# First attention: the last head's values projected two units later, early output tiles begun two units later with two parts in each unit

## The chip, the cores and the metric

The kernel runs on one core of one Trainium2 chip. The metric is the device time of one execution in microseconds (us). TensorE (PE), VectorE (DVE), ScalarE (ACT) and GpSimd (POOL) run their own instruction lists and wait for one another on semaphores; SyncE (SP) issues the loads.

## The reference, cut to what matters

The reference computes two transformer layers with feed-forward halves, on 256 context and 256 latent tokens of width 1024, and then a third layer of another kind. In order: half FFN, differential attention, half FFN; half FFN, grouped attention, half FFN; FFN, a layer with dilated and block attention, FFN. The change touches the attention parts, the first above all:

```python
q, k, v = project(h); qc, kc, vc = project(hc)
q, k = apply_rope(q, cos, sin), apply_rope(k, cos, sin)
k_all = concatenate([kc, k], axis=1); v_all = concatenate([vc, v], axis=1)
sc = einsum('blhid,bkhid->bihlk', qb, kb) * scale        # two maps i for each of 8 heads
p = softmax(sc, axis=-1)
p = p[:, 0] - lam_full * p[:, 1]
o = einsum('bhlk,bkhd->blhd', p, vb)
o = rmsnorm(o, subln) * (1.0 - lambda_init)
y = o @ w_out
```

## The kernel before, in words

All weights stream from HBM once, as tiles of 128 x 1024 f32, through a ring of 6 slots. ScalarE copies each tile to a rounded `w_hi` (L796), GpSimd subtracts to get `w_lo` (L776), and every product is three matmuls, hi x hi, lo x hi and hi x lo (L1589, L1590, L1593). A load into a slot waits until the tile six places earlier has been used.

The first attention (kind "da") has 24 items, q, k and v of 8 heads, one weight tile each, 8 chunks of k. An item is projected in four parts of two chunks (6 matmuls over 512 tokens). There are 32 units, four for each head, one for each block of 128 queries: blocks of latents attend to 512 keys (long), blocks of the context to 256 (short). Heads 0 to 6 take them long, short, long, short; the last head takes two long and then two short ones. Unit U goes through these steps:

- S(U), L1905: scores of the two maps on TensorE, into the same two PSUM banks for every unit, so S(U) waits until the exponentials of U-1 are done. VectorE takes the maximum (L1505) and scales it (L1507), ScalarE the exponentials (L1055).
- C(U), L1408 to L1420: VectorE combines the two maps to `pcomb`.
- T(U), L1918: TensorE transposes `pcomb`, ScalarE copies it to `probT` (L1061).
- PV(U), L1938: TensorE multiplies by the values.
- After a head's units: O (square on ScalarE L1073, `o_raw` on VectorE L1519), oss (sum of squares on TensorE L1968, its root on ScalarE), on (L1536, `o_hi` L1088) and ol (`o_lo`, L1540).

A projected item is evacuated by ScalarE (L1028); q and k then need a rope, rot on TensorE (L1873) and three operations on VectorE (L1475 to L1478); v needs vtr, transposes on TensorE (L1879) and a copy on VectorE to `v_st` (L1482). ScalarE's evacuation of tile t is followed by the `w_hi` copy of tile t+4.

`mixer_plan` (L139) writes one list for an attention before anything is issued, and every engine goes through this list in the same order. Step U of its loop puts down T(U-2), C(U-1), S(U), PV(U-2), and between them projection parts, as many as `QUOTA[kind][U]` says, in thirds: ahead of S, ahead of PV, after PV. Where a unit has no projection part, it places as many early parts as `FILLS[kind][U]` says: two chunks of the output projection of output tiles 0 and 1 (kind "early"), whose sums are left open in PSUM banks 0 and 1. These are also the banks of the items, so the first early part waits for evacuations (L1943). A rope or a transpose is put down when the planner's clock, one tick for each part, has reached its due time, or at the latest ahead of the S or PV that needs it. The list before, from unit 24 (for L1905 and the others each name is one step; `k7.4` is the part of item k, head 7, chunks 4 and 5; `E02` is the early part of output tile 0, chunks 2 and 3; `E06` and `E16` are one chunk each):

```
24: T22 C23 ol4 | q7.4 | S24 | q7.6 | PV22
25: T23 C24 | k7.0 | S25 | k7.2 | rot q7 | PV23 O5 | k7.4
26: T24 C25 | k7.6 | oss5 | S26 on5 | v7.0 | PV24 | v7.2 | rot k7
27: T25 C26 ol5 | v7.4 | S27 | v7.6 | PV25
28: T26 C27 | E00 | S28 | PV26
29: T27 C28 | E10 | vtr v7 | S29 | PV27 O6
30: T28 C29 | E02 | S30 | E12 | oss6 | PV28
31: T29 C30 | E04 | S31 on6 | E14 | PV29 ol6 O7
32: T30 C31 | E06 | PV30
33: T31 | E16 | oss7 on7 ol7 | PV31 O7'
```

T28 and T29 on ScalarE are each followed by the `w_hi` copy of output tile 4 and 5. After the list comes the output projection. The second attention ("ga", 12 items, of which the last is q of head 7 with a norm whose squares ScalarE makes, L1021) and the third ("b2", 30 items) use the same planner.

Of the kernel before, what the change touches and what calls it, by code (L numbers as in the profile page):

```python
# [131 lines left out]

GA_ORDER = [("k", 0), ("v", 0), ("q", 0), ("q", 1), ("k", 1), ("q", 2), ("v", 1)] + [("q", h) for h in range(3, GA_HEADS)]
LEAD = {"da": 4, "ga": 9}
QUOTA = {"da": [3, 3, 3, 3] + [3, 3, 2] * 8, "ga": [2, 2, 3, 3, 3] + [2] * 7}
FILLS = {"da": [0] * 28 + [1, 1, 2, 2, 1, 1], "ga": [0] * 12 + [2, 2, 1, 1, 1, 1], "b2": [0] * 21 + [3, 3, 3, 3, 3]}


def mixer_plan(kind, t0):  # L139
# [51 lines left out]
    order, turns, ropes, norms, clock, pending = [], 0, 0, 0, 0, []  # L191
# [42 lines left out]
    def add_part(part):  # L234

        nonlocal clock
        add("proj", part)
        clock += 1
        it, _, k1 = part
        if k1 == CH:  # L240
            if it["norm"] or it["rope"] or it["what"] == "v":
                pending.append(("ss" if it["norm"] else "rot" if it["rope"] else "vtr", it, clock + (1 if it["norm"] else 2)))

    def prepare(n):
        op, it, _ = pending.pop(n)
# [28 lines left out]
    every = sorted((it for st in sets for it in st["items"]), key=lambda it: it["idx"])  # L274
# [29 lines left out]
    for U in range(len(units) + LAG):  # L304
# [4 lines left out]
        if u:  # L309
            st = u["set"]  # L310
            n, nu = U - st["first_unit"], len(st["units"])
            if kind == "b2":
                nxt = parts(st["s"] + 1)
                mine = nxt[n * len(nxt) // nu:(n + 1) * len(nxt) // nu]
            elif U < len(QUOTA[kind]):
                mine, stream = stream[:QUOTA[kind][U]], stream[QUOTA[kind][U]:]
        fills = FILLS[kind][U] if not mine else 0
        third = -(-len(mine) // 3)
# [45 lines left out]
def build(nc, A):  # L364
# [97 lines left out]
    ident, rot = tab[:, 0:128], tab[:, 128:256]  # L462
# [1114 lines left out]
    def _(pe):  # L1577
# [246 lines left out]
        def mixer(b):  # L1824
            kind = b["kind"]
            S = MS[kind]
            order, n_items, n_first = plans[kind]
# [16 lines left out]
            for op, x, turn in order:  # L1844
                if op == "first":
                    first_phase(b, [(it["t"], item_bank(it, n_first), it["tok"]) for it in x])
                elif op == "proj":
                    x, k0, k1 = x
# [13 lines left out]
                elif op == "ss":  # L1862
                    pe.wait_ge(S["proj_evac"], x["idx"] + 1)
                    turn_wait(turn)
                    mm(psum[:, TURN[turn % 2], x["tok"]], ones[:, :], n_sq[:, x["sq"] % 2, x["tok"]], start=True, stop=True)\
                        .then_inc(S["turn_ready"], 1)
                elif op == "rot":
                    if x["norm"]:
                        pe.wait_ge(S["normed"], x["norm_n"])
                    else:  # L1870
                        pe.wait_ge(S["proj_evac"], x["idx"] + 1)
                    turn_wait(turn)
                    mm(psum[:, TURN[turn % 2], 0:SEQ], rot, latents(x), start=True, stop=True).then_inc(S["turn_ready"], 1)  # L1873
                elif op == "vtr":
                    pe.wait_ge(S["proj_evac"], x["idx"] + 1)
                    turn_wait(turn)
                    src = item_stage(x)
                    for kt in range(width(x["tok"]) // 128):
                        last = nc.tensor.transpose(psum[:, TURN[turn % 2], kt * 128:(kt + 1) * 128],  # L1879
                                                   src[:, kt * 128:(kt + 1) * 128], ident)  # L1880
                    last.then_inc(S["turn_ready"], 1)
                elif op == "S":
                    U, st, n = x["U"], x["set"], x["keys"]
                    if U == 0:
                        pe.wait_ge(S["proj_evac"], n_first)
                    for it in st["q"] + st["k"]:
                        if U == st["first_unit"]:
                            item_ready(it)
                    if kind == "b2":
                        if U >= 2:  # L1890
                            pe.wait_ge(S["biased"], freed[U - 2])
                        biased += len(st["v"])
                        freed[U] = biased
                    elif U >= lag_of(kind):
                        pe.wait_ge(S["exp_done"], exps_through(kind, U - lag_of(kind)))
                    out = scores_of(kind, x)
                    if kind == "ga":
                        q = latents(st["q"][0])[:, x["qt"] * 128 - CTX:x["qt"] * 128 - CTX + 128]
                        k0 = place_of(st["k"][0])
                        last = mm(out, q, k_st[:, k0:k0 + n], start=True, stop=True)  # L1900
                    elif kind == "da":
                        for m in range(2):
                            rows = slice(64 * m, 64 * m + 64)
                            q0, k0 = place_of(st["q"][0]) + x["qt"] * 128, place_of(st["k"][0])
                            last = mm(out[:, m, :], q_st[rows, q0:q0 + 128], k_st[rows, k0:k0 + n], start=True, stop=True)  # L1905
                    else:
                        queries = (q_st, q_odd)[x["j"]]
                        for g in range(len(st["v"])):
                            q0, k0 = place_of(st["q"][g]) + x["qt"] * 128, place_of(st["k"][g])
                            last = mm(out[:, g * n:g * n + n], queries[:, q0:q0 + 128], k_st[:, k0:k0 + n],  # L1910
                                      start=True, stop=True)
                    last.then_inc(S["s_ready"], 1)
                elif op == "T":
                    u, a, e = x
                    pe.wait_ge(S["pc_ready"], u["U"] + 1)
                    turn_wait(turn)
                    for n in range(a, e):
                        last = nc.tensor.transpose(psum[:, TURN[turn % 2], (n - a) * 128:(n - a + 1) * 128],  # L1918
                                                   pcomb[:, u["U"] % 2, n * 128:(n + 1) * 128], ident)
                    last.then_inc(S["turn_ready"], 1)  # L1920
                elif op == "PV":
                    st, U = x["set"], x["U"]
                    done = x["turns"] + [it["turn"] for it in st["v"]]
                    for bank in range(2):
                        if any(n % 2 == bank for n in done):
                            pe.wait_ge(*turn_freed(S, max(n for n in done if n % 2 == bank)))
                    if U == st["first_unit"] and st["s"]:
                        if kind == "ga":
                            if st["s"] > 1:
                                pe.wait_ge(S["olo_ready"], st["s"] - 1)  # L1930
                        elif kind == "da":
                            pe.wait_ge(S["o_evac"], st["s"])
                            pe.wait_ge(S["osq_ready"], st["s"])
                        else:
                            pe.wait_ge(S["olo_ready"], st["s"])
                    for n, (g, kt) in enumerate(x["blocks"]):
                        half = FULL if kind != "da" else LAT if x["qt"] >= 2 else slice(0, CTX)
                        last = mm(psum[:, pv_bank(kind, st["s"], half), x["ocol"]:x["ocol"] + 128], v_tile(st["v"][g], kt),  # L1938
                                  probT[:, U % 2, n * 128:(n + 1) * 128], start=n == 0, stop=n == len(x["blocks"]) - 1)
                    last.then_inc(S["pv_ready"], 1)  # L1940
                elif op == "early":
                    d, k0, k1 = x
                    if d + k0 == 0:  # L1943
                        pe.wait_ge(S["proj_evac"], n_items)
                    if kind == "b2":
                        t = b["t_body"] + 30 + d
                        last = blocks(t % RING if k0 else split(t), psum[:, d, 0:SEQ], normed(FULL_U), range(k0, k1), first=k0,
                                      start=k0 == 0, stop=k1 == CH)
                        if k1 == CH:
                            last.then_inc(tile_used, 1)  # L1950
                    else:
                        t = b["t_out"] + d
                        pe.wait_ge(S["olo_ready"], k1)
                        tok = b["tok_out"]
                        bank = next(bank for j, _, bank in b["pieces"] if j == d)
                        blocks(t % RING if k0 else split(t), psum[:, bank, tok],
                               lambda k: (o_hi[:, k, tok], o_lo[:, k, tok]), range(k0, k1), first=k0, start=k0 == 0, stop=False)
                elif op == "oss":
                    if x["n"] < DA_HEADS:
                        oss((op, x, turn))  # L1960
# [151 lines left out]
```

## Time and profile before

| | |
|---|---|
| median of 3 runs | 2390.12 us (2389.14 to 2393.72) |
| profiled execution | 2389.94 us |
| its span | 2388.1 us |
| PE busy, share of the span | 2315.0 us (97%) |
| PEld, DVE, ACT, POOL busy | 2069.3, 1306.9, 974.7, 1338.8 us |
| first attention's PV steps | 461.3 to 647.7 us of the span |

The span reaches from the first to the last instruction of the profiled execution. A row of the timeline has its start, its duration, engine, source line, output and inputs, and in brackets the idle time of the engine ahead of it and who ended that. Matmuls overlap, so the pitch from one start to the next is what one costs, not its duration.

### The profile page before, as it was taken

The page shows a single profiled execution, that of the slowest core. Times are in us where ns is not written, and L with a number is a line of the kernel's source. Part 1 is how long each engine was busy: PE and PEld are TensorE (multiplying, and loading weights), DVE is VectorE, ACT ScalarE, POOL GpSimd, SP SyncE. Part 2 cuts the span into 40 slices and gives each one's busy share as a digit, 9 for nine tenths or more (in the row PEclk, how much of TensorE's full clock was granted, in tenths as well). Part 3 has the DMA queues.
Part 4 walks back from the last instruction along what each step waited for, and adds up shares of the span by engine and source line. Part 5 has one row for each costly group of instructions (what it writes and reads, how often), then busy time and mean ns, then how long its engine had stood idle before and what let it go on. Part 6 is the DMA issues. An engine that isn't in the chain of part 4 may idle for free.

```text
span 2388.1 us, 36102 instructions
## 1 busy us (share of the span) xinstructions
PE 2315.0 (97%) x14528; PEld 2069.3 (87%) x14528; DVE 1306.9 (55%) x2196; ACT 974.7 (41%) x1605; POOL 1338.8 (56%) x700
## 2 busy tenths in 40 slices
PE   7999999999889999999999999899999999999998
PEld 5888889777688888899888897799999999999998
DVE  8898296666678982967332036564324315533331
ACT  4322224455442322244223235455445444555443
POOL 4564465222135654654444443178878887468886
PEclk9999999999999999999999999999999999999999
DMA  6555362211025553624553331145545564345554
GB/s 271 212 190 180 110 219 85 71 62 54 28 79 212 194 177 110 219 94 178 194 176 110 97 102 62 45 158 185 179 149 196 176 188 163 106 152 184 183 178 134
DMA packets 97509, 350.09 MB, mean 147 GB/s; under 512 B 10945, under 2 KB 10945, under 8 KB 96961
## 3 DMA queue, kind: packets, MB, share of 16 engines
q1 hardware_dynamic: 97344, 347.81, 43.2%
q8 instruction: 115, 1.88, 0.3%
q14 instruction: 50, 0.40, 0.1%
HBM read 346.71 MB, written 1.05 MB: 146 GB/s over the span
## 4 chain that ended last, share of the span: by engine, by line
PE 60%; DVE 5%; ACT 2%; issue 2%; DMA 1%; POOL 1%; SPq 0%; DVEq 0%; ACTq 0%
PE psum L1589 19%; PE psum L1593 19%; PE psum L1590 19%; POOL w_lo L776 1%; ACT w_hi L796 1%; PE psum L1938 1%; DMA w_raw<-in_ffn_out 0%; DVE stat L1505 0%; DVE psum L1141 0%; DVE psum L1221 0%; DVE h L1227 0%; PE psum L1910 0%; DVE pcomb L1414 0%; DVE u_lo L1445 0%; ACT prob L1055 0%
## 5 line engine op out<-in xcount | busy, mean ns | idle before, releaser
L776 POOL TENSOR_TENSOR w_lo<-w_raw,w_hi 128x1024 fp32r<-128x1024 f32 (+3 forms) x696 | 1338.6, 1945 | 1032.3 <-ACT w_hi L796 1031.7
L1589 PE MATMUL psum<-u_hi,w_hi 128*128 128x256 f32 (+2 forms) x2912 | 973.9, 334 | 12.1 <-POOL w_lo L776 8.2
L1593 PE MATMUL psum<-u_lo,w_hi 128*128 128x256 f32 (+2 forms) x2912 | 948.7, 326 | 3.3 <-DVE u_lo L1213 2.0
L1590 PE MATMUL psum<-u_hi,w_lo 128*128 128x256 f32 (+2 forms) x2912 | 947.4, 325 | 0.0
L796 ACT ACTIVATE w_hi<-w_raw 128x1024 fp32r<-128x1024 f32 (+1 forms) x522 | 537.3, 1032 | 439.9 <-PE psum L1593 345.1
L1589 PEld LDWEIGHTS psum<-u_hi,w_hi 128*128 128x128 f32 x2912 | 555.2, 191 | 75.3 <-issue 24.4
L1593 PEld LDWEIGHTS psum<-u_lo,w_hi 128*128 128x128 f32 x2912 | 554.6, 190 | 51.8 <-DVE u_lo L1213 3.8
L1590 PEld LDWEIGHTS psum<-u_hi,w_lo 128*128 128x128 f32 x2912 | 555.5, 191 | 45.3 <-issue 3.4
L1589 PE MATMUL psum<-gu_hi,w_hi 128*128 128x256 f32 (+1 forms) x1188 | 379.3, 319 | 1.0 <-POOL w_lo L776 1.0
L1590 PE MATMUL psum<-gu_hi,w_lo 128*128 128x256 f32 (+1 forms) x1188 | 378.2, 318 | 0.0
L1593 PE MATMUL psum<-gu_lo,w_hi 128*128 128x256 f32 (+1 forms) x1188 | 378.1, 318 | 0.0
L1589 PEld LDWEIGHTS psum<-gu_hi,w_hi 128*128 128x128 f32 x1188 | 226.3, 191 | 17.0 <-issue 1.4
L1590 PEld LDWEIGHTS psum<-gu_hi,w_lo 128*128 128x128 f32 x1188 | 226.3, 191 | 15.8
L1593 PEld LDWEIGHTS psum<-gu_lo,w_hi 128*128 128x128 f32 x1188 | 226.3, 191 | 15.4
L1141 DVE CUSTOM_DVE_ANT_0 psum<-ada_hi,silu_c,col 128x1024 f32<-128x1024 f32 x80 | 155.4, 1942 | 54.6 <-DMA ada_hi<-in_ada_w 50.8
L948 ACT ACTIVATE sq<-psum 128x512 f32<-128x512 f32 x66 | 39.5, 598 | 324.7 <-PE psum L1593 175.1
L1141 DVE CUSTOM_DVE_ANT_0 psum<-ada_lo,silu_c,col 128x1024 f32<-128x1024 f32 x80 | 148.6, 1857 | 33.2 <-DMA ada_lo<-in_ada_w 28.7
L1318 DVE TENSOR_TENSOR gu_lo<-sq,gu_hi 128x512 fp32r<-128x512 f32 (+1 forms) x132 | 147.1, 1115 | 18.3 <-ACT gu_hi L933 18.3
L1350 DVE TENSOR_TENSOR sq<-sq,psum 128x512 f32<-128x512 f32 (+1 forms) x110 | 63.7, 579 | 162.3 <-PE psum L1593 157.2
L1237 DVE TENSOR_TENSOR rstd<-rstd,sq 128x256 f32<-128x256 f32 (+1 forms) x58 | 45.1, 778 | 182.1 <-ACT sq L892 90.2
L1141 DVE CUSTOM_DVE_ANT_0 psum<-ada_out,silu_c,col 128x1024 f32<-128x1024 f32 x64 | 134.8, 2168 | 0.1
L1055 ACT ACTIVATE prob<-psum,stat 128x512 f32<-128x512 f32 (+1 forms) x80 | 47.6, 599 | 103.3 <-DVE stat L1507 103.1
(180 smaller groups left out, 1989.2 us busy)
## 6 DMA issues: line engine op xcount, KB each, us to landing
w_raw<-in_ffn_in SPq DMA_DIRECT2D x264, 512.0 KB, 3.5
w_raw<-in_ffn_out SPq DMA_DIRECT2D x96, 448.0 KB, 3.4
ada_hi<-in_ada_w SPq DMA_DIRECT2D x48, 512.0 KB, 5.2
ada_lo<-in_ada_w SPq DMA_DIRECT2D x48, 512.0 KB, 5.2
w_raw<-in_ffn_out SPq DMA_DIRECT2D x48, 512.0 KB, 3.6
ada_out<-in_ada_w SPq DMA_DIRECT2D x32, 512.0 KB, 3.8
w_raw<-in_b_qkv SPq DMA_DIRECT2D x30, 512.0 KB, 3.4
w_raw<-in_da_in SPq DMA_DIRECT2D x24, 512.0 KB, 3.5
```

The costliest lines, as they stand in the source:

```text
L776: last = pool.tensor_tensor(w_lo[:, slot, w], w_raw[:, slot, w], w_hi[:, slot, w].bitcast(F32), ALU.subtract)
L796: scalar.activation(w_hi[:, slot, 0:cols], w_raw[:, slot, 0:cols], ACT.Copy).then_inc(hi_ready, 1)
L948: scalar.activation(s_up[:, j, tok], psum[:, pair_bank(m), tok], ACT.Silu).then_inc(silu_ready, 1)
L1055: scalar.activation(prob[:, U % 2, m * 512:m * 512 + n], src, ACT.Exp, bias=stat[:, U % 4, 2 + m:3 + m], scale=scale, accum_out=stat[:, U ...
L1141: return vec.tensor_tensor_reduce(out=psum[:, junk:junk + 2, :].rearrange("p a b -> p (a b)"), in0=tile, in1=silu_c[:, c, :], scale=1.0, s ...
L1237: vec.tensor_tensor(sqsum[:, tok], sqsum[:, tok], sq[:, i % 2, tok], ALU.add).then_inc(yacc_ready, 1)
L1318: vec.tensor_tensor(gu_lo[:, m, tok], s_up[:, m % 2, tok], gu_hi[:, m, tok].bitcast(F32), ALU.subtract)\
L1350: vec.tensor_tensor(s_up[:, j, tok], s_up[:, j, tok], psum[:, pair_bank(m) + 1, tok], ALU.mult)\
L1589: mm(out, w_hi[:, slot, w], x_hi, start=start and n == 0, stop=False)
L1590: mm(out, w_lo[:, slot, w], x_hi, start=False, stop=False)
L1593: last = mm(out, w_hi[:, slot, w], x_lo, start=False, stop=stop and n == len(ks) - 1)
L1938: last = mm(psum[:, pv_bank(kind, st["s"], half), x["ocol"]:x["ocol"] + 128], v_tile(st["v"][g], kt), probT[:, U % 2, n * 128:(n + 1) * 12 ...
```

## The change

The last two units of projection move from 26 and 27 to 28 and 29, with fewer parts in units 22 to 27; the eight early parts move to units 30 to 33, two in each. The very last item's rope or transpose is due one tick after its last part and not two. The first early part of tile 0 waits for all items but the last, that of tile 1 for all. The last two edits act on all three attentions.

```diff
-QUOTA = {"da": [3, 3, 3, 3] + [3, 3, 2] * 8, "ga": [2, 2, 3, 3, 3] + [2] * 7}
-FILLS = {"da": [0] * 28 + [1, 1, 2, 2, 1, 1], "ga": [0] * 12 + [2, 2, 1, 1, 1, 1], "b2": [0] * 21 + [3, 3, 3, 3, 3]}
+QUOTA = {"da": [3, 3, 3, 3] + [3, 3, 2] * 6 + [2, 3, 2] + [2, 2, 1] + [2, 2], "ga": [2, 2, 3, 3, 3] + [2] * 7}
+FILLS = {"da": [0] * 30 + [2, 2, 2, 2], "ga": [0] * 12 + [2, 2, 1, 1, 1, 1], "b2": [0] * 21 + [3, 3, 3, 3, 3]}
...
-                pending.append(("ss" if it["norm"] else "rot" if it["rope"] else "vtr", it, clock + (1 if it["norm"] else 2)))
+                pending.append(("ss" if it["norm"] else "rot" if it["rope"] else "vtr", it, clock + (1 if it["norm"] or it is every[-1] else 2)))
...
                 elif op == "early":
                     d, k0, k1 = x
-                    if d + k0 == 0:
-                        pe.wait_ge(S["proj_evac"], n_items)
+                    if k0 == 0:
+                        pe.wait_ge(S["proj_evac"], n_items - 1 + d % 2)
```

## Rows read from the trace of the kernel before

**Rows 1.** The page: busy time of TensorE and the others, share of the span, instructions.

```profile
PE 2315.0 (97%) x14528; PEld 2069.3 (87%) x14528; DVE 1306.9 (55%) x2196; ACT 974.7 (41%) x1605; POOL 1338.8 (56%) x700
```

**Rows 2.** Windows at the first attention's end: length, busy us (instructions) of PE, PEld, DVE, ACT, POOL.

```profile
582.00:620.00 38.00, 38.00 (x190) 27.48 (x188) 24.59 (x52) 20.02 (x46) 9.92 (x4) 1.00 0.18 56
620.00:648.00 28.00, 22.37 (x120) 15.98 (x119) 16.30 (x33) 14.09 (x36) 7.06 (x3) 1.00 0.06 19
```

**Rows 3.** Timeline of TensorE, 620 to 648 us: the four longest waits (start, duration, line).

```profile
621.13 0.50 PE L1589 MATMUL psum<-o_hi,w_hi 128*128 128x512 f32 x1 [1.01 <-ACT vT L1028]
...
631.85 0.70 PE L1905 MATMUL psum<-k_st,q_st 64*128 64x256 f32 x4 [1.35 <-ACT prob L1055]
...
636.76 0.66 PE L1918 MATMUL psum<-tab,pcomb 128*128 128x128 f32 x4 [0.87 <-DVE pcomb L1420]
...
644.27 0.50 PE L1589 MATMUL psum<-o_hi,w_hi 128*128 128x512 f32 x1 [2.15 <-DVE o_lo L1540]
```

**Rows 4.** Timeline of TensorE, 602 to 611 us: steps of units 25 and 26, read as pitches.

```profile
602.81 0.70 PE L1905 MATMUL psum<-k_st,q_st 64*128 64x256 f32 x4
603.44 0.50 PE L1589 MATMUL psum<-u_hi,w_hi 128*128 128x512 f32 x1
...
604.94 0.59 PE L1873 MATMUL psum<-q_st,tab 128*128 128x256 f32 x2
605.37 0.61 PE L1938 MATMUL psum<-probT,v_st 128*128 128x128 f32 x4
...
607.56 0.48 PE L1589 MATMUL psum<-u_hi,w_hi 128*128 128x512 f32 x1
...
609.04 1.02 PE L1968 MATMUL psum<-o_sq,ones 128*128 128x512 f32 x2
609.99 1.13 PE L1905 MATMUL psum<-k_st,q_st 64*128 64x512 f32 x4
611.05 0.50 PE L1589 MATMUL psum<-u_hi,w_hi 128*128 128x512 f32 x1
```

**Rows 5.** Timeline of VectorE, 615 to 637 us: a rope, two combinations, a copy, an o_raw.

```profile
615.46 0.42 DVE L1475 TENSOR_TENSOR rope_a<-k_st,tab 128x256 f32<-128x256 f32 x1 [1.60 <-PE psum L1873]
...
616.26 0.42 DVE L1478 TENSOR_TENSOR k_st<-rope_a,rope_b 128x256 f32<-128x256 f32 x1
...
617.38 0.75 DVE L1420 SCALAR_TENSOR_TENSOR pcomb<-prob,stat 128x512 f32<-128x512 f32 x1
...
628.30 0.68 DVE L1482 COPY v_st<-psum 128x512 f32<-128x512 f32 x1
...
632.38 0.75 DVE L1519 TENSOR_SCALAR o_raw<-psum,col 128x512 f32<-128x512 f32 x1 [2.06 <-ACT o_sq L1073]
...
633.83 2.88 DVE L1420 SCALAR_TENSOR_TENSOR pcomb<-prob,stat 128x512 f32<-128x512 f32 x1
```

**Rows 6.** Timeline of GpSimd: one subtraction by itself, two in a row.

```profile
633.80 2.36 POOL L776 TENSOR_TENSOR w_lo<-w_raw,w_hi 128x1024 fp32r<-128x1024 f32 x1 [9.34 <-ACT w_hi L796]
...
660.15 4.92 POOL L776 TENSOR_TENSOR w_lo<-w_raw,w_hi 128x1024 fp32r<-128x1024 f32 x2 [16.48 <-ACT w_hi L796]
```

**Rows 7.** Timeline of ScalarE, 619 to 632 us: exponentials, evacuation, weight copy, exponentials, square.

```profile
619.57 0.47 ACT L1055 ACTIVATE prob<-psum,stat 128x256 f32<-128x256 f32 x1 [3.51 <-DVE stat L1507]
...
620.49 0.59 ACT L1028 ACTIVATE vT<-psum 128x512 f32<-128x512 f32 x1
620.96 1.06 ACT L796 ACTIVATE w_hi<-w_raw 128x1024 fp32r<-128x1024 f32 x1
...
630.35 0.69 ACT L1055 ACTIVATE prob<-psum,stat 128x512 f32<-128x512 f32 x1 [3.27 <-DVE stat L1507]
...
631.69 0.59 ACT L1073 ACTIVATE o_sq<-psum 128x512 f32<-128x512 f32 x1
```

**Rows 8.** Timeline of TensorE in the second attention: its first early part.

```profile
1531.17 0.39 PE L1589 MATMUL psum<-o_hi,w_hi 128*128 128x256 f32 x1 [1.28 <-ACT n_sq L1021]
```

**Rows 9.** Timeline of VectorE in the third attention, unit 21: the last values' copy.

```profile
2097.42 0.42 DVE L1482 COPY v_st<-psum 128x256 f32<-128x256 f32 x1
```

## Prediction

> **What bounds the kernel now.** I read the page's busy shares first: TensorE is busy for 2315.0 of 2388.1 us [rows 1], at full clock. A change that only reorders work can win at most TensorE's idle time near the reordered steps. So next, the windows around the end of the first attention: from 582 to 620 us TensorE has no idle time at all; from 620 to 648 us it is busy 22.37 of 28.00 us, so 5.6 us are idle [rows 2]. Then the timeline of TensorE there: four waits make most of it [rows 3]. The first early output part waits 1.01 us for the evacuation of the last head's values (all 24 items must be evacuated); S(30) waits 1.35 us for the exponentials of unit 29; T(29) waits 0.87 us for pcomb(29); the early part (0, 6..7) waits 2.15 us for head 6's low half. Thus 5.6 us is the whole prize here: 0.23% of the run.
>
> **What the change does to the order.** With the new quotas (2,3,2,2,2,1,2,2 parts in units 22 to 29) the planner's loop gives, written as in the list of the order before (E06 is the early part of tile 0 from k=6): unit 26 is T24 C25 | k7.2 | rot q7 | S26 | k7.4 | oss5 | PV24; unit 27 is T25 C26 | k7.6 | S27 | on5 | PV25; unit 28 is T26 C27 ol5 | v7.0 | rot k7 | S28 | v7.2 | PV26; unit 29 is T27 C28 | v7.4 | S29 | v7.6 | PV27 O6; unit 30 is T28 C29 | E00 | vtr v7 | S30 | E10 | oss6 | PV28; unit 31 is T29 C30 | E02 | S31 | on6 | E12 | PV29 ol6 O7; unit 32 is T30 C31 | E04 | E14 | oss7 on7 ol7 | PV30; and the last is T31 | E06 | E16 | PV31 O7', before the output. No instruction is added or removed on any engine. Four parts leave units 22 to 27; units 28, 29, 32 and 33 hold two parts each instead of one. The last key head's rope now comes right ahead of S28, which needs it; before, it came in unit 26.
>
> **Units 22 to 27: 6.0 us earlier.** One part takes 1.50 us after an S (603.44 to 604.94) and 1.48 elsewhere (607.56 to 609.04) [rows 4]. Walking the list with those pitches (S 0.63 on two key tiles, 1.06 on four, rot 0.43, oss 0.9), T26 comes at 613.5 instead of 619.5. The softmax chain keeps up: exponentials last 0.92 us (two key tiles) or 1.34 (four) [rows 7], and each is done 0.3 us or more before the next S. T24 to T26 find pcomb ready. So 4 x 1.5 us is carried to unit 28, as work still to be done.
>
> **Unit 28: a new wait.** v7.0 and rot k7 end at 615.8. S28 needs k7's rope, and VectorE has C27 and ol5 queued in front of it. C27 needs exp27. Those stand behind k7.6's evacuation and the head copy of a weight tile on ScalarE (0.60 and 1.06 us) [rows 7]: they run 614.05 to 615.1. That same copy releases a w_lo subtraction on GpSimd of 2.4 us, 614.1 to 616.5, or to 616.85 if on5 holds it up first. Here is a row that decides much: pcomb(29) took 2.88 us instead of 0.75 [rows 5], and ended just after GpSimd's w_lo, which ran 633.80 to 636.16 [rows 6]. An operation of VectorE with its operands in SBUF waits for GpSimd. So C27 stands until 616.85, ends at 617.7; ol5 takes 0.65, the rope 1.2 [rows 5], and S28 starts at 619.55. TensorE idles 3.7 us. Bounds: without GpSimd in the way C27 ends at 616.1, S28 starts at 618.0 and the idle is 2.1; the rope can't be avoided. I take 3.7, since the copy always stands directly ahead of exp27, and 2.4 us outlast the 1.0 us of exp27.
>
> **Units 29 and 30: a second new wait.** S28 619.55, v7.2, PV26, T27 623.0, v7.4, S29 624.7 (exp28 ends 623.6), v7.6 to 627.3, PV27. On ScalarE: exp29 627.3 to 628.8, evacuation of v7 to 629.3, weight copy to 630.35, o_sq6 to 630.8, probT28, a second copy to 632.35. GpSimd so runs two w_lo back to back, 630.4 to 635.3. T28 at 627.75, E00 (now waiting for 23 items only; free), vtr v7 at 629.65, S30, E10, oss6: TensorE has work to 633.2. But VectorE takes o_raw6 (0.75 us [rows 5], ends 631.5), C29, and only then the copy of v7's transposes, which PV28 needs. C29's four operations need SBUF: the first gets in between the two w_lo, the rest wait for 635.3 and end 636.4; the copy takes 0.68 [rows 5] to 637.05. PV28 starts then, 3.8 us idle. If all of C29 slips in between the two w_lo, PV28 starts at 634.85: 2.2 us less. With GpSimd out of the way in both units PV28 starts near 632.05, 5.0 us less.
>
> The page of the Trainium skill "SBUF — State Buffer", section "Who interferes with whom", calls the shared port pair an exclusive lock, held for the whole instruction by whoever issues first. The trace agrees: two w_lo took 4.92 us without a gap to speak of [rows 6]. By that rule C29's waiting operation goes first, the second w_lo next, and the others behind it, which is the 636.4 above; were the port shared by bandwidth instead, C29 would end near 634 and the sum would be some 2.2 us lower.
>
> **Units 31 to 33.** PV28 637.05, T29 637.95, E02, S31 639.9 (exp30 ends 638.9), E12, PV29 642.0, T30 642.9, E04, E14, oss7 646.0, PV30, T31 646.85 (C31 ends 646.7), E06, E16 to 648.5. ol6 is blocked to 644.6 by a third w_lo, as in the trace, but E06 is now late enough: the 2.15 us wait goes. The 0.87 and 1.35 waits go too. PV31 waits for probT31 behind oss7's two activations and o_hi7: 648.7. The output starts at 649.1, against 647.7; as o_sq of the last piece is ready in time, the fifth chunk starts at 650.9, which is 0.8 us late against the trace. Counted by idle time it is more: 3.7 + 3.8 + 0.2 after, less the 5.6 before, is 2.1; the pitches that I rounded down lie between. I take **+1.0 us**: what the filler covers in units 30 to 33 it uncovers in 28 and 30. The rest of the output is the same list; its tile loads (two of them after tiles 0 and 1 are released) move with it.
>
> **The other two attentions.** The first early part's wait is relaxed in all three. In the second attention it waits 1.28 us for q7's squares [rows 8]; now it runs at once (0.82 us of matmuls, to 1530.5), and the sum of squares behind it waits for them instead, until 1531.15 and not 1531.99: **-0.8 us**, bounds 0 (if a chain behind it is bound elsewhere) and -0.84. In the third, nothing waits there. The rule for the last values' transpose ("due one step sooner") acts there too: v5's transposes pass S(21), so VectorE's copy of 0.42 us [rows 9] now precedes that unit's softmax; that delay finds slack except behind exp23, where PV22 already waits for probT: **+0.3 us**, bounds 0 and 0.42.
>
> Sum: 1.0 - 0.8 + 0.3 = +0.5 us on the profiled execution's 2389.94 us (its span of 2388.1 and 1.8 around it): 2390.4. The median of the three runs is 2390.12, 0.2 above that execution, so the forecast is 2390.6 us. The three runs differ by 4.6 us among themselves, and 0.2% is 4.8 us: a smaller change can hardly be told from none.
>
> **Rivals.**
> A. GpSimd costs less than I take. For it: only one pcomb in the four units of the tail is caught in the trace, the rest escape. Against: both copies stand right ahead of the exponentials. With the second collision softened 2390.6 - 2.2 = 2388.4; with both gone (PV28 at 632.05) 2390.6 - 5.0 = 2385.6.
> B. Slower. In unit 27 the scaling of the maximum (a two-element operation in SBUF) starts at 613.8, GpSimd's w_lo at 614.1. If it comes 0.3 us later it stands until 616.5, exp27 ends 617.5, S28 starts 620.55: +1.0, so 2391.6. It decides once S27 slips by 0.3 us against k7.6's evacuation; for it, the margin is so small; against, both hang on the same last matmul of k7.6.
> C. The waits simply fill: two parts in each of the last units cover the chains, nothing new waits, and the 5.6 us idle go but for 0.5: 2390.1 - 5.1 - 0.5 = 2384.5. Against it: the rope right ahead of S28.
> D. The reordering has no effect and only the relaxed wait counts: 2389.3. The quotas do move v7, so this is thin.
>
> **Chances.** Forecast 0.48, A 0.25, B 0.18, C 0.07, D 0.02. Faster by over 0.2% needs C or the far end of A: 0.09. Slower by over 0.2% needs B and a further 3.5 us: 0.05. Within 0.2%: 0.86. Range: A's near end and some of its far end, B and the runs' own spread above: 2386.5 to 2393.0.
>
> **What will show it.** Right if the trace has: T26 near 613.5; an idle of 2 to 4 us ahead of S28, released by the rope's last addition on VectorE; one of 2 to 4 us ahead of PV28, released by v_st's copy, with C29 stretched; no wait ahead of E06; in the second attention E00 starting before 1530 and the sum of squares waiting for n_sq. Wrong if S28 starts without a wait, if PV28 finds v7 ready, or if units 22 to 27 show an idle of their own, which would mean that the parts taken out of them were cover.

## The result: 0.18% slower, and the profile after

| | before | after |
|---|---|---|
| median, 12 runs each | 2389.24 us | 2394.54 us |
| lowest to highest | 2386.84 to 2393.72 | 2390.47 to 2396.26 |
| ratio, 95% interval | | 1.0018 [1.0010, 1.0026] |
| profiled execution | 2389.94 us (span 2388.1) | 2396.26 us (span 2394.4) |
| mean granted clock of the profiled execution | 0.997 | 0.994 |

The forecast was 2390.6 us (2386.5 to 2393.0), most likely "within 0.2%". The time is 5.3 us over before and 1.5 us above the range. A second build of the changed kernel, run later, gave 2394.3 us (1.0020 [1.0011, 1.0029]).

The profile's busy line answers to [rows 1]. TensorE does the same 14528 matmuls and is "busy" 5.8 us longer.

```profile
PE 2320.8 (97%) x14528; PEld 2073.1 (87%) x14528; DVE 1302.9 (54%) x2196; ACT 975.0 (41%) x1605; POOL 1340.5 (56%) x700
```

That is the first hint: reordering alone would show as idle time, not as busy time. The windows show where. Columns as in [rows 2]; the seventh value behind the window's name, after the five engines, is the granted clock (1.00 is 2.4 GHz, 0.50 is 1.2 GHz).

```profile
620.00:648.00 28.00, 22.76 (x93) 16.14 (x94) 14.50 (x26) 10.34 (x22) 6.33 (x3) 0.82 0.05 19
622.00:624.00 2.00, 2.00 (x5) 0.50 (x5) 0.14 (x1) 0.00 (x0) 0.00 (x0) 0.50 0.03 8
624.00:626.00 2.00, 2.00 (x5) 1.57 (x6) 1.25 (x2) 0.68 (x2) 0.00 (x0) 0.50 0.00 0
626.00:628.00 2.00, 2.00 (x10) 1.85 (x9) 1.13 (x4) 0.77 (x4) 0.00 (x0) 0.52 0.00 0
628.00:630.00 2.00, 2.00 (x12) 1.46 (x13) 0.35 (x1) 0.39 (x1) 0.00 (x0) 1.00 0.00 0
640.00:642.00 2.00, 0.23 (x1) 0.24 (x2) 1.97 (x4) 0.00 (x0) 0.04 (x1) 0.89 0.00 0
642.00:644.00 2.00, 2.00 (x10) 2.00 (x11) 0.84 (x5) 1.45 (x5) 0.00 (x0) 0.50 0.00 0
644.00:646.00 2.00, 2.00 (x10) 1.61 (x8) 0.71 (x2) 1.97 (x4) 0.00 (x0) 0.76 0.00 0
```

Before, this window stood at 1.00 with 120 matmuls [rows 2]; now it holds 93 in about the same busy time. The clock is at 0.50 from about 621 to about 628 us, so it fell while TensorE was still waiting, and again from about 642 to 645.

What TensorE did before each fall is in its timeline. It answers to [rows 3]: none of the four waits of before is left, and two of 3.5 us are new. (S, T, PV and E are the steps of the list.)

```profile
617.63 0.59 PE L1873 MATMUL psum<-k_st,tab 128*128 128x256 f32 x2
621.74 2.08 PE L1905 MATMUL psum<-k_st,q_st 64*128 64x512 f32 x4 [3.52 <-DVE k_st L1478]
623.75 0.80 PE L1589 MATMUL psum<-u_hi,w_hi 128*128 128x512 f32 x1
624.35 0.63 PE L1590 MATMUL psum<-u_hi,w_lo 128*128 128x512 f32 x1
...
626.48 1.74 PE L1938 MATMUL psum<-probT,v_st 128*128 128x128 f32 x8
628.05 0.38 PE L1918 MATMUL psum<-tab,pcomb 128*128 128x128 f32 x2
...
641.76 2.08 PE L1938 MATMUL psum<-probT,v_st 128*128 128x128 f32 x8 [3.50 <-DVE v_st L1482]
643.63 1.06 PE L1918 MATMUL psum<-tab,pcomb 128*128 128x128 f32 x4
...
646.21 0.70 PE L1905 MATMUL psum<-k_st,q_st 64*128 64x256 f32 x4
```

S(28) takes 2.08 us where S(29), of the same shape, takes 1.13. From the start of S(28) to T(27) it is 6.31 us (621.74 to 628.05); in a kernel below with the same list and a full clock there it is 3.43 (fill28, 621.21 to 624.64). From PV(28) to S(31) it is 4.45 us, against 2.92 (fill_full, 638.47 to 641.39). That is 2.9 and 1.5 us, 4.4 together.

VectorE and GpSimd show who made the waits. They answer to [rows 5] and [rows 6].

```profile
617.37 0.17 DVE L1408 RECIPROCAL stat<-stat 128x2 f32<-128x2 f32 x1 [0.49 <-ACT prob L1055]
617.57 1.55 DVE L1416 TENSOR_TENSOR stat<-stat,small 128x1 f32<-128x1 f32 x1
...
636.71 1.05 DVE L1416 TENSOR_TENSOR stat<-stat,small 128x1 f32<-128x1 f32 x1
637.68 2.64 DVE L1417 TENSOR_SCALAR prob<-prob,stat 128x512 f32<-128x512 f32 x1
640.36 0.75 DVE L1420 SCALAR_TENSOR_TENSOR pcomb<-prob,stat 128x512 f32<-128x512 f32 x1
```

```profile
616.37 2.75 POOL L776 TENSOR_TENSOR w_lo<-w_raw,w_hi 128x1024 fp32r<-128x1024 f32 x1 [8.53 <-ACT w_hi L796]
635.35 4.68 POOL L776 TENSOR_TENSOR w_lo<-w_raw,w_hi 128x1024 fp32r<-128x1024 f32 x2 [16.24 <-ACT w_hi L796]
```

A multiplication of one element in each partition, in combination 27 (L1416, 0.16 us alone), ends at 619.12, where the first subtraction ends. In combination 29 the second operation ends 0.3 us after the 640.03 at which the two subtractions end.

In the second attention the wait of [rows 8] is gone and a shorter one stands behind it. In the third, the wait of PV(22) is 0.77 us and was 0.64. After:

```profile
1537.04 0.60 PE L1918 MATMUL psum<-tab,pcomb 128*128 128x128 f32 x4
...
1538.93 0.70 PE L1865 MATMUL psum<-n_sq,ones 128*128 128x256 f32 x2 [0.57 <-ACT n_sq L1021]
...
1542.61 0.66 PE L1918 MATMUL psum<-tab,pcomb 128*128 128x128 f32 x4 [0.52 <-DVE pcomb L1414]
...
1548.85 0.39 PE L1589 MATMUL psum<-o_hi,w_hi 128*128 128x256 f32 x1 [1.54 <-DVE o_lo L1524]
...
2110.52 0.71 PE L1938 MATMUL psum<-probT,v_st 128*128 128x128 f32 x4 [0.77 <-ACT probT L1061]
```

The second attention before:

```profile
1529.29 0.60 PE L1918 MATMUL psum<-tab,pcomb 128*128 128x128 f32 x4
...
1541.10 0.39 PE L1589 MATMUL psum<-o_hi,w_hi 128*128 128x256 f32 x1 [1.55 <-DVE o_lo L1524]
```

From the transpose ahead of the relaxed wait to the early part that waits for `o_lo` it is 11.81 us before and 11.81 after. What the relaxed wait gains there, a new wait of 0.52 us for pcomb and the steps around it give back.

**A ruler for the stretch.** Short falls of the clock come in all these kernels at other places too, in the trace of before for instance around 1446 and 1776 us, and they move the end of a run by some us. So I measure the changed stretch by itself: from the start of S(22) to the first operation of the output (`MEMSET rstd`, L1377). Before and after:

```profile
583.54 1.13 PE L1905 MATMUL psum<-k_st,q_st 64*128 64x512 f32 x4
```
```profile
652.83 0.48 DVE L1377 MEMSET rstd<- 128x512 f32 x1
```
```profile
585.13 1.13 PE L1905 MATMUL psum<-k_st,q_st 64*128 64x512 f32 x4
```
```profile
660.00 0.48 DVE L1377 MEMSET rstd<- 128x512 f32 x1
```

That is 69.3 us before and 74.9 after: +5.6 us.

### The profile page after: what moved, and what is told of

Its sections match the earlier page's. It is cut to its first block, busy times and chain, and to the rows that moved or that the text cites. A ratio compares the mean times of both kernels' runs of the same rounds, so it can differ in the third digit from the quotient of the medians.

```text
span 2394.4 us, 36101 instructions
## 1 busy us (share of the span) xinstructions
PE 2320.8 (97%) x14528; PEld 2073.1 (87%) x14528; DVE 1302.9 (54%) x2196; ACT 975.0 (41%) x1605; POOL 1340.5 (56%) x700
## 3 DMA queue, kind: packets, MB, share of 16 engines
HBM read 346.71 MB, written 1.05 MB: 145 GB/s over the span
## 4 chain that ended last, share of the span: by engine, by line
PE 61%; DVE 4%; ACT 2%; issue 1%; POOL 1%; DMA 1%; DVEq 0%; SPq 0%; ACTq 0%
PE psum L1589 20%; PE psum L1593 20%; PE psum L1590 19%; ACT w_hi L796 1%; POOL w_lo L776 1%; PE psum L1938 1%; DVE stat L1505 0%; DVE psum L1221 0%; PE psum L1910 0%; DVE h L1227 0%; DVE pcomb L1414 0%; DVE u_lo L1445 0%; ACT prob L1055 0%; PE psum L1918 0%; DMA w_raw<-in_ga_in 0%
## 5 line engine op out<-in xcount | busy, mean ns | idle before, releaser
L1141 DVE CUSTOM_DVE_ANT_0 psum<-ada_out,silu_c,col 128x1024 f32<-128x1024 f32 x64 | 129.3, 2083 | 0.1
```

What stands on the lines that cost most here:

```text
L1141: return vec.tensor_tensor_reduce(out=psum[:, junk:junk + 2, :].rearrange("p a b -> p (a b)"), in0=tile, in1=silu_c[:, c, :], scale=1.0, s ...
```

## The experiments

The runs were timed in four sets. The medians of the kernel before, in the same sets, were 2389.90, 2389.38, 2389.38 and 2389.58 us. "Stretch" is the ruler above; "clock" says whether the granted clock fell to 0.50 in it.

| kernel | median us | ratio [95%] | wait S(28), PV(28), us | stretch, us | clock |
|---|---|---|---|---|---|
| before_again | 2389.76 | 0.9999 [0.9990, 1.0008] | 0, 0 | 69.3 | no fall |
| after_again | 2394.30 | 1.0020 [1.0011, 1.0029] | 3.52, 3.52 | 73.7 | two falls |
| quota_only | 2397.12 | 1.0028 [1.0018, 1.0039] | 3.52, 3.89 | 77.6 | two |
| wait_only | 2387.97 | 0.9989 [0.9981, 0.9998] | 0, 0 | 69.7 | one |
| fill28 | 2393.59 | 1.0014 [1.0005, 1.0023] | 0.63, 3.50 | 70.5 | no fall |
| fill_both | 2394.50 | 1.0016 [1.0007, 1.0025] | 0.63, 0.63 | 70.5 | no fall |
| fill_both_again | 2393.62 | 1.0017 [1.0008, 1.0026] | 0.62, 0.61 | 70.5 | no fall |
| fill_full | 2393.11 | 1.0013 [1.0004, 1.0022] | 0.18, none | 70.5 | no fall |
| late_k7 | 2390.21 | 1.0003 [0.9994, 1.0013] | 2.11, 3.52 | 73.3 | two |
| late_v7 | 2390.46 | 1.0007 [0.9998, 1.0016] | 3.52, 0 | 69.6 | one |
| late_copies | 2386.71 | 0.9989 [0.9980, 0.9998] | 2.12, 0 | 68.2 | one |
| late_copies_again | 2386.92 | 0.9990 [0.9982, 0.9999] | 2.11, 0 | 66.7 | no fall |
| late_fill | 2386.46 | 0.9985 [0.9977, 0.9994] | 0.33, 0 | 66.7 | no fall |
| late_before | 2389.74 | 0.9999 [0.9990, 1.0008] | 0, 0 | 70.0 | one |

after_again is the changed kernel without an edit. Expected of it were a time 4 to 5 us over before and, if the falls belong to the waits, both falls again; both came.

**1. Is it the clock? Fillers in the waits (fill28, fill_both, fill_both_again, fill_full).** `keep_clock` issues dummy matmuls of 0.24 us each on TensorE.

```diff
                 elif op == "S":
                     U, st, n = x["U"], x["set"], x["keys"]
+                    if kind == "da" and U == 28:
+                        keep_clock(0, 13)
...
                 elif op == "PV":
                     st, U = x["set"], x["U"]
+                    if kind == "da" and U == 28:      # not in fill28
+                        keep_clock(SUMS, 13)
```

> The changed kernel with 13 matmuls of ones (128 columns, 0.24 us a call, 3.2 us in all, into a PSUM bank that nothing uses then) put ahead of S28, inside its wait of 3.5 us. Clock theory: the changed kernel lost 2.8 us because TensorE's granted clock fell to 0.5 after the idle ahead of S28, and 1.6 us in the same way ahead of PV28. With the first wait filled the clock stays at 1.00 through S28, v7.2 and PV26, S28 takes 1.13 us and not 2.08, and the time falls by 2.8 us against the changed kernel, to about 2391.7. Rival, the waits alone: the loss is the 7 us of waits; filling one with work that does nothing changes nothing (2394.5), and the slow matmuls would be slow for another reason.

> The same with 13 more such matmuls ahead of PV28, into the sums' bank, inside its wait of 3.5 us. Clock theory: granted clock 1.00 from 616 to 660 us, 4.4 us less than the changed kernel, about 2390.1, which is what the forecast without a clock loss gave. Rival, the waits alone: 2394.5 still.

> The kernel with fillers ahead of S28 and PV28 once more. Its first median stood 3.7 us over the kernel before, against 1.4 us by the chain of the first attention alone (its stretch was 1.9 us longer in the trace, 4.2 less than in the changed kernel's). Clock theory: it must now lie between, 2 to 4 us under the changed kernel measured beside it. Rival: the falls are exchanged for others elsewhere or hardly occur outside of the trace, and it lies within 1 us of the changed kernel.

> The changed kernel with 15 filler matmuls instead of 13 ahead of S(28) and ahead of PV(28), so that only some 0.2 us of idle time is left at each instead of 0.63. If what is left of the clock's cost hangs on that remaining idle time: the time falls from 2393.6 to 2394.5 us (13 fillers) toward 2390 us. If the fillers bring back the clock but the work still ends late, because the idle time itself is the larger part: 2393 to 2394.5 us again, with a mean granted clock of 0.996 to 0.9965 over the executions as before the change. Longer by over 0.3 us would say that the fillers themselves stand in the way.

The window of fill_full, and its S(28):

```profile
620.00:648.00 28.00, 27.69 (x161) 21.48 (x160) 17.68 (x33) 12.38 (x29) 7.55 (x3) 1.00 0.06 19
```
```profile
621.31 1.13 PE L1907 MATMUL psum<-k_st,q_st 64*128 64x512 f32 x4 [0.18 <-DVE k_st L1478]
```

In the window the clock is 1.00, and S(28) takes 1.13 us. In all four filler traces the stretch is 70.5 us, within 0.03 of one another. The fillers stand inside waits that are there anyway, so this is the change with the clock taken out: 70.5 - 69.3 = **1.2 us**. The rest of the 5.6 us in the profiled execution, 4.4 us, is the clock; in after_again it is 3.2. The mean granted clock over the executions comes back as well: 0.9953 with the change (23 executions), 0.9964 with fillers (45), 0.9967 before (129).

The executions give a second price for the clock. Among the executions of one kernel, 0.001 less of the mean granted clock goes with about 1.3 us more (a straight line through all of them). By this estimate the 0.0014 between before and after are worth 1.8 us; they would be 3.3 us (0.0014 of 2390 us) if all the clock that was lost had been needed. The two traces, with 3.2 and 4.4 us, lie at that upper end and above it.

The medians do not follow. With fillers they lie from 0.2 us above to 1.2 us below the changed kernel's 2394.30, where the expectations of fill28 and fill_both had 2.8 and 4.4 us; even by the estimate above the clock that came back is worth 1.4. By what was written down ahead of these runs, the rival ("the waits alone") has the times, and the clock theory has the traces. fill_full, with 15 fillers, shows that it does not hang on the 0.6 us left idle. One way in which the gain is given back is in the trace of fill_full: just behind the stretch, VectorE's norm meets two subtractions of GpSimd, TensorE waits 3.69 us, and its clock falls to 0.50 there.

```profile
665.08 2.43 DVE L1237 TENSOR_TENSOR rstd<-rstd,sq 128x256 f32<-128x256 f32 x1 [3.61 <-PE psum L1593]
```
```profile
668.00:672.00 4.00, 4.00 (x19) 4.00 (x20) 0.63 (x2) 0.00 (x0) 0.00 (x0) 0.50 0.00 0
```

The same wait is 1.3 to 1.5 us long before and after the change, with no fall behind it in those four traces; in fill_both_again it is 1.79, with a fall. The other two filler traces have neither a wait over 1.6 us nor a fall there, and still their rest of the run takes 1737.3 and 1736.4 us where the changed kernel's takes 1734.4. The mean of the 45 filler executions is 3.8 us over before's, where the idle time (1.2 us here and 0.3 in the third attention) and 0.4 to 0.7 us of clock add up to 2.2 at most. So why the fillers' times stay high is open.

Behind the stretch there is one more fall that the ruler does not see. All 16 traces have a wait of 2.5 to 2.6 us ahead of a norm's sum of squares (L1623, L1627 where lines were added; at 708.9 us in before). In 11 of them a fall follows, in both traces of the changed kernel too, and the 100 us behind the stretch are then 1.2 to 1.7 us longer than in before; in the two traces of before none follows. Whether that is chance or comes with the change, two traces cannot say.

**2. Is the trace of before typical (before_again)?** The same kernel.

> The kernel before, unchanged, for a second trace of it. The stretch from the first half FFN's end to the first attention's end took 358.0 us in the first trace. If that trace was typical: 357 to 359.5 us again and no slow clock within 600 to 660 us. If it was a lucky draw: over 359.5 us, and the part of the loss that idle time explains shrinks by the same amount. Time 2389 to 2390.5 us, ratio 1.000.

The stretch is again 69.3 us, with no fall, and has the same waits within 0.03 us. The +1.2 rests on two traces against four. The time and the stretch came as the first branch expected.

**3. Who makes the waits? The weight copies moved (late_copies).** ScalarE's `w_hi` copies of output tiles 2 to 5 are taken from behind the evacuations of k7 and v7 and from behind T(28) and T(29), and put behind the exponentials of units 28 and 30 and behind T(29) and T(30). GpSimd's subtractions go with them.

```diff
                         scalar.activation(dst, src, ACT.Copy).then_inc(S["proj_evac"], 1)
+                if kind == "da" and x["idx"] >= 22:
+                    return
                 refill(x["t"])
...
+                    if kind == "da" and U in (28, 30):
+                        heads_to(b["t_out"] + {28: 2, 30: 3}[U])
...
-                    if kind == "da" and u["set"]["s"] == DA_HEADS - 1:
-                        heads_to(min(b["t_out"] + 4 + u["U"] - u["set"]["first_unit"], b["t_out"] + RING - 1))
+                    if kind == "da" and u["U"] in (29, 30):
+                        heads_to(b["t_out"] + {29: 4, 30: 5}[u["U"]])
```

> The changed kernel with four of ScalarE's weight copies moved (and so GpSimd's subtractions): output tile 2's from k7's evacuation to behind the exponentials of unit 28, tile 3's to behind those of unit 30, tiles 4 and 5's behind probT29 and probT30. Theory: GpSimd held C27 (first SBUF pair operation 1.55 us instead of 0.16) and C29 (1.05 + 2.64 us instead of 0.16 + 0.48). Without that, S28 waits 2.1 us instead of 3.5 and PV28 0.5 instead of 3.5; if the clock stays up after waits that short, the time falls by 4.4 + 4.4, to about 2386; if it still falls ahead of S28, to about 2388.5. Rival: the order itself (rope and copy behind the combination) makes the waits, and they stay over 3 us each: 2394.5.

> The changed kernel with all four weight copies moved, a second time. If the first result (2386.7 us, 0.9989 of before) was the kernel and not the draw of the clock: 2386 to 2388 us, ratio under 1.0 again, S(28) waits 2.1 us for the rope, PV(28) does not wait. If it was the draw: near before, 2389.5 us.

VectorE in the second trace: combination 27, the rope's last addition, combination 29 and the copy of the values.

```profile
615.70 0.16 DVE L1420 TENSOR_TENSOR stat<-stat,small 128x1 f32<-128x1 f32 x1
615.78 0.34 DVE L1421 TENSOR_SCALAR prob<-prob,stat 128x256 f32<-128x256 f32 x1
...
617.95 0.42 DVE L1482 TENSOR_TENSOR k_st<-rope_a,rope_b 128x256 f32<-128x256 f32 x1
...
629.79 0.16 DVE L1420 TENSOR_TENSOR stat<-stat,small 128x1 f32<-128x1 f32 x1
629.87 0.48 DVE L1421 TENSOR_SCALAR prob<-prob,stat 128x512 f32<-128x512 f32 x1
...
631.05 0.68 DVE L1486 COPY v_st<-psum 128x512 f32<-128x512 f32 x1
```

And what TensorE still waits for:

```profile
618.47 1.13 PE L1909 MATMUL psum<-k_st,q_st 64*128 64x512 f32 x4 [2.11 <-DVE k_st L1482]
...
643.51 0.44 PE L1922 MATMUL psum<-tab,pcomb 128*128 128x128 f32 x2 [1.67 <-DVE pcomb L1424]
```

No operation of the combinations is held, PV(28) finds its values, and what is left ahead of S(28) is the rope itself, 2.11 us. The stretch is 66.7 us without a fall, 2.5 under before; the median is 7.6 and 7.4 us below the changed kernel's 2394.3, and 3.2 and 2.5 below before. So the two waits that GpSimd makes, with what follows them, are more than the whole loss.

**4. One collision or two (late_k7, late_v7)?** late_k7 moves the copy of tile 2 alone, late_v7 those of tiles 3 to 5 alone. The edit of late_k7:

```diff
+                if kind == "da" and x["idx"] == 22:
+                    return
                 refill(x["t"])
...
+                    if kind == "da" and U == 28:
+                        heads_to(b["t_out"] + {28: 2}[U])
```

> Only the weight copy of output tile 2 is moved, from k7's evacuation to behind the exponentials of unit 28; the other copies stay as in the changed kernel. Theory (two separate collisions with GpSimd, each followed by a slow clock if the idle time is long): the wait ahead of S(28) falls from 3.5 to about 2.1 us, pcomb(27) runs 0.75 us instead of 1.55 and unstretched by GpSimd; the wait ahead of PV(28) stays at 3.5 us with two subtractions in a row. Time 1.4 us below the changed kernel if the clock is unaffected, up to 4 us below where the clock no longer falls behind S(28): 2390.5 to 2393 us against 2394.3. Rival (one collision carries all): if this one, 2387; if the other, no change, 2394.3.

> Only the weight copies of output tiles 3, 4 and 5 are moved, from v7's evacuation and from behind units 28 and 29 to behind the exponentials of unit 30 and T(29), T(30); tile 2's copy stays where the changed kernel has it. Theory: the wait ahead of S(28) stays at 3.5 us; the wait ahead of PV(28) falls from 3.5 us to under 1 us, since combination 29 no longer stands behind GpSimd; 3 us less from idle time and up to 1.6 us from the clock: 2389.7 to 2391.3 us. Rival (the k7 collision carries all): 2394. The sum of this gain and that of the kernel with tile 2's copy alone should be near the 7 us that moving all gave.

They take 4.1 and 3.8 us off the changed kernel's 2394.3; together that is 7.9, and moving all took 7.4 to 7.6. Two separate collisions, about equal, and both needed. The stretch without a fall is 70.5 with both and 66.7 with neither, 3.8 us in idle time. The other half of the 7.5 us of the medians is beyond idle time. The clock's 3.2 to 4.4 in the traces would cover it; by the mean granted clock (0.9968 in the 22 executions with all copies moved, 0.9953 with the change) it is 2 us, up to 3.5. In late_k7's trace, too, the clock falls twice:

```profile
620.74 1.54 PE L1909 MATMUL psum<-k_st,q_st 64*128 64x512 f32 x4 [2.11 <-DVE k_st L1482]
639.45 2.07 PE L1942 MATMUL psum<-probT,v_st 128*128 128x128 f32 x8 [3.52 <-DVE v_st L1486]
```

**5. Which edit does it (quota_only, wait_only)?** quota_only is the kernel before with the two lines `QUOTA` and `FILLS` of the change; wait_only is the kernel before with the relaxed wait of the early parts alone:

```diff
-                    if d + k0 == 0:
-                        pe.wait_ge(S["proj_evac"], n_items)
+                    if k0 == 0:
+                        pe.wait_ge(S["proj_evac"], n_items - 1 + d % 2)
```

> The kernel before with the new quotas and fills alone: the early parts wait for all items, the last values' transpose is due two steps later. Against the changed kernel the first early part then waits 1.3 us for v7's evacuation and the transposes come behind S30 and E10; PV28 waits for the same C29 and 0.7 us longer, and the second attention keeps its 0.8 us wait: 1.0 to 1.5 us slower than the changed kernel, some 6 us slower than before. Rival, that one of the two small edits is what made the change slower: this one lies within 2 us of the kernel before.

> The kernel before with only the relaxed wait of the early parts (tile 0: all items but the last; tile 1: all). Theory: 0.8 us less in the second attention, and the 1.01 us wait of the first early part in the first attention goes, of which S28's chain may take some back: 1.0 to 1.8 us less than before, about 2387.8. Rival, the wait matters only where the profile names it last and is taken up by the next one: no change, 2389.2.

The quotas alone cost 7.7 us by the medians and 6.7 by the ratio (7 executions, interval 4.3 to 9.3). The waits of quota_only:

```profile
620.77 2.08 PE L1905 MATMUL psum<-k_st,q_st 64*128 64x512 f32 x4 [3.52 <-DVE k_st L1478]
633.30 0.50 PE L1589 MATMUL psum<-o_hi,w_hi 128*128 128x512 f32 x1 [1.03 <-ACT vT L1028]
641.49 2.08 PE L1938 MATMUL psum<-probT,v_st 128*128 128x128 f32 x8 [3.89 <-DVE v_st L1482]
```

The relaxed wait alone gains 1.9 us, and the two small edits get back 2.8 us of the quotas' loss by the medians, 1.9 by the ratios. They are good edits under a bad one, though not where they were forecast to be. In the trace of wait_only the early part E06 comes 0.8 us sooner behind S(22) than before (59.9 and 60.7 us), and in the second attention, from transpose to early part, it is again 11.8 us: nothing gained. The rest of the 1.9 us can be the draw of the clock, whose mean was 0.9974 in these executions and 0.9967 before.

**6. Candidates for a version that beats both (late_fill, late_before).** late_fill is late_copies with one line more, `keep_clock(0, 8)`, ahead of S(28); late_before is wait_only with the copies of late_copies.

> All four copies moved, and 8 filler matmuls on TensorE, some 1.9 us, into PSUM bank 0 ahead of S(28), in the 2.1 us that it waits for the last key head's rope. If a slower clock behind that wait costs something in part of the executions: up to 1.5 us below the kernel without the fillers, near 2386 us. If the wait is too short for that: the same as the kernel without them, within 0.5 us. If the fillers lengthen the wait because their last one ends after the rope: up to 0.3 us slower.

> The kernel before with the relaxed wait and with the four weight copies moved as in late_copies. Theory: wait_only's gain (about 1.9 us) plus the 0.87 us that T29 waits for a pcomb that GpSimd holds up, and up to 1.0 us of the wait for head 6's low half: 3 to 4 us under the kernel before, about 2386. Rival, the copies only move the collisions to other operations of VectorE: the same as wait_only.

late_fill is the fastest kernel of the study, 2.9 us (0.15%) under before and 7.8 under the changed kernel. Of the 2.9, the new order with the copies moved gives 2.5 to 3.2. The fillers' own part, 0.5 us, is not resolved; its stretch without a fall is the same 66.7. late_before, expected near 2386 us, gains nothing over before in the median, and its stretch is no shorter than that of wait_only (70.0 and 69.7 us, one fall in each): the moved copies help only with the new quotas.

## Why the prediction was wrong

**What held.** The walk through the list did. S(28) waits 3.52 us for the rope (predicted 3.7) and PV(28) 3.50 for the values' copy (3.8), both through combinations held by GpSimd; PV(31) waits 0.24 us for probT (0.2); no wait ahead of E06, S(30) or T(29). The first attention's term, +1.0, measures +1.2 once the clock is out of it; that the sum of new waits and carried work comes out so near owes something to luck, for "+1.0" was chosen between sums that did not agree. The third attention's +0.3 measures +0.33: from L1496 at 2090.85 us to L1529 at 2106.75 VectorE takes 15.9 us before and in all five traces without the edit of the due time, and 16.2 in all eleven with it. T(26) is at 615.8, but this execution was 1.6 us late already at S(22): against the 6.0 us earlier of the prediction it is 5.3. Most of the difference is a wait that the prediction named as a sign of being wrong, "an idle of their own" in units 22 to 27: T(21), the first step of unit 23, waits 0.51 us in the trace of after (at 590.53) and does not wait in that of before.

**The step that failed** is "Unit 28: a new wait" together with "Units 29 and 30: a second new wait". It priced each wait at its length and ran the steps behind it at the pitches of [rows 4], which all come from full clock. Behind these waits TensorE ran at 1.2 GHz, and S(28), v7.2, PV(26), PV(28), T(29) and E02 took up to twice as long: 4.4 us in the profiled execution, 3.2 in the second trace.

A second term failed beside it: the second attention's -0.8 measures 0.0 (11.81 us before and after). The prediction had this bound, 0 "if a chain behind it is bound elsewhere", and took the other.

With both the sum is 1.2 + 0.0 + 0.3 at full clock, +1.5, and the clock on top of it: 3.2 to 4.4 us by the two traces, +4.7 to +5.9 in all; 1.8 to 3.3 by the mean granted clock of the executions, +3.3 to +4.8. Measured are 4.9 and 5.3 us between the medians, and 4.4 between the means (23 executions with the change, 129 before).

The first paragraph had the clock in hand ("at full clock") but took it as given. In the stretch the longest wait of before, 2.15 us, had no fall behind it. But the longest wait of the whole trace of before, 2.89 us at 1446 us, had one, and the prediction did not look there:

```profile
1445.97 1.22 PE L1623 MATMUL psum<-sq,ones 128*128 128x256 f32 x2 [2.89 <-DVE sq L1194]
```
```profile
1446.00:1448.00 2.00, 2.00 (x7) 1.82 (x8) 0.00 (x0) 0.74 (x2) 0.00 (x0) 0.50 0.00 0
```

So the trace of before already showed that a new wait of 3.7 us puts the clock at risk. The page of the Trainium skill "TensorE: Matmul & The Clock Gate", section "Why this matters for your kernels", warns of idle gaps between bursts of matmuls because the clock then falls to half rate. Eight of the nine waits of 3.5 to 3.9 us in these traces agree with it and one does not.

**The rivals.** A (GpSimd costs less) is refuted: both collisions cost what was said. B had the right sign and the wrong mechanism; the scaling of the maximum in unit 27 was not caught (0.17 us at 616.11, the subtraction starts at 616.37). C fell with the waits. D fell too, though its relaxed wait is real: alone it is worth 1.9 us, but in the first attention, where it takes away the 1.01 us of [rows 3], and not in the second.

**What is shown, and what is not.** Shown: the quotas cause the loss; what GpSimd adds to the two waits is more than the loss, since moving its subtractions takes 7.5 us off; the clock falls behind the waits and costs 3.2 to 4.4 us of the stretch in the two traces; with a full clock the change costs 1.2 us there. Supported, not shown by itself: that the clock is the larger part of the median's loss. The moved copies and the lower mean granted clock speak for it; the fillers' medians speak against it, and why is open.

## What to carry to other kernels

A wait of TensorE is not priced by its length alone: in a kernel that is 97% busy, a wait of 3.5 us was mostly followed by 3 to 7 us at half clock, which cost 1.5 to 2.9 us more in the traces. Look through the trace that you have for waits of that size and for what the clock did behind them, before you price a new one. When a step is moved next to its consumer, ask what VectorE has queued in front of it and which weight copy on ScalarE will start GpSimd at that moment; moving those copies was worth more than the reordering. Measure a small change by a stretch between two fixed instructions of the trace, which here repeats within 0.03 us as long as the clock does not fall in it, where whole runs scatter by several us; and then measure what lies behind the stretch too.

## What the runs showed of the hardware

- The clock falls behind long waits often, but not always. In the changed stretch, of nine waits of 3.5 to 3.9 us ahead of S(28) or PV(28), eight were followed by a granted clock of 0.50; the ninth, in fill28, was not. Of seven waits of 2.1 to 2.3 us, four were. Of eight cut to under 0.7 us by fillers, none. Elsewhere in the run the wait of 2.9 us (at 1446 us in before) stands in 15 of the 16 traces with a fall behind 12, and the one of 2.5 to 2.6 us at 709 us in all 16 with a fall behind 11.
- The price of a fall goes with its length. From S(28) to S(29) it is 5.1 us without a fall (fill28), 6.7 to 6.8 with the clock down for some 3.4 us (after_again, late_k7, late_v7, late_copies), and 7.9 to 8.0 with some 6.8 (quota_only, after). A fall can begin behind the first step: after_again's S(28) still took 1.13 us.
- GpSimd can hold a combination more than once: between two back-to-back subtractions VectorE got one tiny operation through (L1416, ended at 637.76), and the next was held for the whole second one. The page of the Trainium skill "SBUF — State Buffer", section "Who interferes with whom", says that whoever issues first has the port for its whole instruction; the rows above agree, 1.05 and 2.64 us where 0.16 and 0.48 are the durations alone.
- Not every operation of VectorE with its operands in SBUF is held, as the prediction had it. The reciprocal of combination 27 took 0.17 us at 617.37, in the middle of GpSimd's subtraction of 616.37 to 619.12.
